# Query transposes two heads at a time, with the second copy of the rows made on GpSimd

## What is computed

```python
D_MODEL = 1024; SEQ = 1024; HEAD_DIM = 64
NSA_HEADS = 8; NSA_KV_HEADS = 2
...
def hybrid_layer(x, norm_w, w_in, q_norm_w, k_norm_w, cmp_k_pos, cmp_k_w1, cmp_k_b1, cmp_k_w2,
                 cmp_v_pos, cmp_v_w1, cmp_v_b1, cmp_v_w2, conv_w, conv_b, w_out):
    h = rms_norm(x, norm_w)
    proj = jnp.einsum('bsd,de->bse', h, w_in)
    q, kv_all, gate_logits, nsa_z, cv_h, cv_b, cv_c, cv_z = jnp.split(proj, SPLIT_POINTS, axis=-1)
    q = apply_rope(rms_norm(q.reshape(B_, S_, NSA_HEADS, dh), q_norm_w), pos)
    k_c, v_c, k_s, v_s, k_w, v_w = [t.reshape(B_, S_, G, dh) for t in jnp.split(kv_all, 6, axis=-1)]
    ...
        s_c = jnp.einsum('bgqrd,bcgd->bgqrc', qb, k_c).astype(jnp.float32) * scale
        p_c = masked_softmax(s_c, ...)
        o_cmp = jnp.einsum('bgqrc,bcgd->bgqrd', p_c.astype(v_c.dtype), v_c)
        ...
        s_s = jnp.einsum('bgqrd,bgqnld->bgqrnl', qb, k_g).astype(jnp.float32) * scale
        ...
        s_w = jnp.einsum('bgqrd,bkgd->bgqrk', qb, k_wb).astype(jnp.float32) * scale
    ...
    o_nsa = (gates[..., 0:1] * unblock(o_cmp) + gates[..., 1:2] * unblock(o_slc)
             + gates[..., 2:3] * unblock(o_win))
    o_nsa = o_nsa.reshape(B_, S_, D_NSA) * jax.nn.silu(nsa_z)
    u = cv_c * cv_h
    conv = lax.conv_general_dilated(u, conv_w[:, None, :], ...) + conv_b
    o_conv = cv_b * conv * jax.nn.silu(cv_z)
    mix = jnp.concatenate([o_nsa, o_conv], axis=-1)
    return x + jnp.einsum('bse,ed->bsd', mix, w_out)
```

## Time and profile before

| | us |
|---|---|
| median of 3 runs | 647.09 |
| lowest and highest | 646.69, 647.68 |
| the profiled execution | 648.53 |
| its span, first to last instruction | 646.7 |

### The profile page before, as it was taken

The page is one execution under the profiler, slowest core; times in us unless marked ns, Lnnn a source line. Parts: engine busy times, 40 slices in busy tenths (PEclk is TensorE's granted clock), DMA queues, the critical chain, the costliest instruction groups (busy, mean ns, idle before and its releaser), DMA issues.

```text
span 646.7 us, 10319 instructions
## 1 busy us (share of the span) xinstructions
PE 635.9 (98%) x3513; PEld 532.9 (82%) x3513; DVE 486.4 (75%) x1153; ACT 377.4 (58%) x872; POOL 203.8 (32%) x220
## 2 busy tenths in 40 slices
PE   9999999999999999999999999999999999999997
PEld 6889998888888888888877888877878888787875
DVE  4955979996745754776788867897988778888853
ACT  6754457564354444555666656668766656665651
POOL 2543304343323322423224222348742221312210
PEclk9999999999999999999999999999999999999999
DMA  8523111112111111111111010123311101011111
GB/s 299 178 57 116 34 33 50 49 35 82 32 50 33 50 33 33 36 32 34 32 34 33 17 33 18 36 89 122 116 49 56 43 34 66 33 33 50 49 34 66
DMA packets 20212, 37.35 MB, mean 58 GB/s; under 512 B 2880, under 2 KB 4288, under 8 KB 20160
## 3 DMA queue, kind: packets, MB, share of 16 engines
q1 hardware_dynamic: 20016, 36.68, 18.2%
q10 hardware_dynamic: 144, 0.00, 0.0%
HBM read 32.48 MB, written 4.19 MB: 57 GB/s over the span
## 4 chain that ended last, share of the span: by engine, by line
PE 79%; DVE 14%; issue 2%; ACT 2%; POOL 1%; DMA 1%; SPq 0%; ACTq 0%; DVEq 0%
PE pf L1478 10%; PE pf L1479 9%; PE pf L1480 9%; PE tp L1792 5%; PE sc L1632 4%; PE sc L1631 4%; PE po L1769 4%; PE po L1770 4%; PE pj L1478 3%; PE pj L1479 3%; PE pj L1480 3%; PE sc L1478 3%; PE sc L1479 3%; PE sc L1480 3%; DVE sc L1377 2%
## 5 line engine op out<-in xcount | busy, mean ns | idle before, releaser
L963 ACT CAST pth<-tp 128x512 fp32r<-128x512 f32 (+1 forms) x148 | 86.7, 586 | 102.1 <-PE tp L1792 101.6
L1377 DVE CUSTOM_DVE_ANT_0 sc<-sc,maskb 128x64 f32<-128x64 f32 (+8 forms) x192 | 103.0, 560 | 42.6 <-PE sc L1632 42.0
L1399 DVE TENSOR_TENSOR ptl<-tp,pth 128x512 fp32r<-128x512 f32 x132 | 90.9, 689 | 22.2 <-ACT pth L963 21.8
L683 POOL TENSOR_SCALAR qp<-qp,precip,gate 128x64 f32<-128x64 f32 x64 | 42.3, 661 | 182.3 <-DVE precip L1367 182.2
L643 POOL TENSOR_TENSOR fl<-fraw,fh 128x512 fp32r<-128x512 f32 x40 | 54.5, 1363 | 95.1 <-ACT fh L808 95.1
L1478 PE MATMUL pf<-hh,fh 128*128 128x512 f32 x200 | 80.2, 401 | 0.0
L1479 PE MATMUL pf<-hl,fh 128*128 128x512 f32 x200 | 78.4, 392 | 0.0
L1480 PE MATMUL pf<-hh,fl 128*128 128x512 f32 x200 | 78.2, 391 | 0.0
L634 POOL TENSOR_TENSOR wl<-qp,wh 128x512 fp32r<-128x512 f32 (+1 forms) x33 | 49.5, 1521 | 87.5 <-ACT wh L723 83.8
L1792 PEld LDWEIGHTS tp<-idr,qpr 128*128 128x128 f32 (+1 forms) x592 | 61.6, 137 | 11.9 <-issue 2.4
L1792 PE MATMUL tp<-idr,qpr 128*128 128x128 f32 (+1 forms) x592 | 68.2, 238 | 1.2 <-POOL qp L683 0.6
(11 more groups left out here) (259 smaller groups left out, 1556.8 us busy)
## 6 DMA issues: line engine op xcount, KB each, us to landing
fraw<-in_wside SPq DMA_DIRECT2D x40, 256.0 KB, 2.7
qp<-in_wpack SPq DMA_DIRECT2D x28, 256.0 KB, 3.2
xo<-in_x SPq DMA_DIRECT2D x16, 256.0 KB, 2.7
out<-xo SPq DMA_DIRECT2D x16, 256.0 KB, 2.0
wor<-in_wout SPq DMA_DIRECT2D x12, 256.0 KB, 2.8
mixc<-in_xcm SPq DMA_DIRECT2D x4, 512.0 KB, 7.4
xlow<-in_xcm SPq DMA_DIRECT2D x3, 512.0 KB, 6.8
qp<-in_wpack SPq DMA_DIRECT2D x5, 224.0 KB, 2.7
```

The source lines that it names most:

```text
L963: nc.scalar.copy(pth[ptn % 2][0:r, :], tp[tpn % 2][0:r, :]).then_inc(pth_ready, 1)
L1377: return V.tensor_tensor_reduce(row, row, mask, -1.0, -NEG, ALU.add, ALU.min, most)
L1399: V.tensor_tensor(ptl[ptn % 2][:, :], tp[tpn % 2][:, :], pth[ptn % 2][:, :].bitcast(F32), ALU.subtract).then_inc(tp_read, 1)
```

## The change

Two heads stand side by side in the 128 columns that one transpose turns, so two transposes read the normalised queries where they lie (`qpr`) and give four heads: of each pair the first head comes out in partitions 0 to 63 and the second in 64 to 127. ScalarE casts each half of the partitions into partitions 0 to 63 of `qh` (two casts of 64x256). GpSimd then copies partitions 0 to 63 of `qh` to 64 to 127 (`double_queries`), at the head of step 8u-1 (`unit_at(k, -1)`). `qd_ready` now counts that copy, and the first scores of a unit wait for it. VectorE subtracts in two pieces of 64x256 into partitions 0 to 63 of `ql`; the other half of `ql` is cleared once, before unit 0. `qd` goes. On GpSimd `last` names the semaphore and count of the instruction before the copy: the copy waits until that one is complete, and what follows waits until the copy is complete.

```diff
-                with ExitStack() as f:
-                    qdr = sb("qdr", [P, GH, 2, HD], F32R, f)
-                qd = sb("qd", [P, GH, 2, HD], F32, d)
...
@@ gpsimd
-            def copy_queries(u):
-
-                i, g = UNITS[u]
-                if u >= 1:
-                    pool.wait_ge(q_normed, 2)
-                    pool.wait_ge(qh_ready, u)
-                src = qn[:, i, g * 256:(g + 1) * 256].rearrange("p (h d) -> p h d", h=GH)
-                for twice in range(2):
-                    ins = nc.gpsimd.tensor_copy(qd[:, :, twice, :], src)
-                ins.then_inc(qd_ready, 1)
+            def double_queries(u):
+
+                pool.wait_ge(qh_ready, 2 * u + 2)
+                pool.wait_ge(*last)
+                nc.gpsimd.tensor_copy(qh[HD:P, :, :], qh[0:HD, :, :].bitcast(F32)).then_inc(qd_ready, 1)
+                pool.wait_ge(qd_ready, u + 1)
...
-            pool.wait_ge(q_normed, 1)
-            copy_queries(0)
...
+            last, scaled, low = (fl_ready, 3), 0, 0
+            double_queries(0)
             for k in range(STEPS):
+                if unit_at(k, -1):
+                    double_queries(unit_at(k, -1))
                 s = k - 1
...
-                u = unit_at(k, -5)
-                if u:
-                    copy_queries(u)
...
@@ scalar
-                nc.scalar.copy(qh[:, :, :], tp[tpn % 2][:, :].rearrange("p (h q) -> p h q", h=GH)).then_inc(qh_ready, 1)
+                pairs = qh[:, :, :].rearrange("p (j e) q -> p j e q", e=2)
+                for e in range(2):
+                    src = tp[tpn % 2][e * HD:(e + 1) * HD, 0:2 * P].rearrange("p (j q) -> p j q", j=2)
+                    nc.scalar.copy(pairs[0:HD, :, e, :], src).then_inc(qh_ready, 1)
@@ vector
-                dve.wait_ge(qh_ready, u + 1)
-                V.tensor_tensor(ql[:, :, :], tp[tpn % 2][:, :].rearrange("p (h q) -> p h q", h=GH),
-                                qh[:, :, :].bitcast(F32), ALU.subtract).then_inc(tp_read, 1)
+                pairs_h, pairs_l = (v[:, :, :].rearrange("p (j e) q -> p j e q", e=2) for v in (qh, ql))
+                for e in range(2):
+                    dve.wait_ge(qh_ready, 2 * u + e + 1)
+                    src = tp[tpn % 2][e * HD:(e + 1) * HD, 0:2 * P].rearrange("p (j q) -> p j q", j=2)
+                    ins = V.tensor_tensor(pairs_l[0:HD, :, e, :], src, pairs_h[0:HD, :, e, :].bitcast(F32), ALU.subtract)
+                ins.then_inc(tp_read, 1)
...
+            dve.wait_ge(qh_ready, 1)
+            V.memset(ql[HD:P, :, :].bitcast(F32), 0.0)
             queries(0)
@@ tensor
-                pe.wait_ge(qd_ready, u + 1)
+                pe.wait_ge(q_normed, 1 if u == 0 else 2)
                 if tpn >= 2:
                     pe.wait_ge(tp_read, tpn - 1)
-                for h in range(GH):
-                    ins = nc.tensor.transpose(tp[tpn % 2][:, h * P:(h + 1) * P].bitcast(F32R),
-                                              qdr[:, h, :, :].rearrange("p u d -> p (u d)"), idr[:, :])
+                i, g = UNITS[u]
+                for j in range(2):
+                    o = (8 + i) * 512 + (2 * g + j) * P
+                    ins = nc.tensor.transpose(tp[tpn % 2][:, j * P:(j + 1) * P].bitcast(F32R), qpr[:, o:o + P], idr[:, :])
                 ins.then_inc(tp_done, 1)
...
                 if h == 0 and w % 2 == 0:
+                    pe.wait_ge(qd_ready, w // 2 + 1)
                     pe.wait_ge(tp_read, q_tp[w // 2])
```

The remaining lines of the diff keep `last` up to date behind each GpSimd operation, for instance:

```diff
                 for h in halves_at(k):
                     half_lo(h)
+                    last = fl_ready, h + 1
```

More of the change, by code:

```diff
@@ L445, in hybrid_layer @@
         woh_ready, wol_ready = sem("woh_ready"), sem("wol_ready")
-        qd_ready, qh_ready, kend_ready = sem("qd_ready"), sem("qh_ready"), sem("kend_ready")
+        qh_ready, qd_ready, kend_ready = sem("qh_ready"), sem("qd_ready"), sem("kend_ready")
         s_done, max_ready, exp_done = sem("s_done"), sem("max_ready"), sem("exp_done")
@@ L684, in _ @@
                         .then_inc(cmp_scaled, 1)
-                u = unit_at(k, -5)
-                if u:
-                    copy_queries(u)
+                    scaled += 1
+                    last = cmp_scaled, scaled
                 u = unit_at(k, -6)
@@ L690, in _ @@
                     copy_last_keys(u)
+                    last = kend_ready, u + 1
                 for h in halves_at(k):
                     half_lo(h)
+                    last = fl_ready, h + 1
                 for j in wout_at(k):
@@ L697, in _ @@
                         .then_inc(wol_ready, 1)
+                    last = wol_ready, j + 1
                 m = mixn_half_at(k)
@@ L702, in _ @@
                                             msh[:, 0:4, :].bitcast(F32), ALU.subtract).then_inc(msl_ready, 1)
+                    low += 1
+                    last = msl_ready, low
                 m = mixc_half_at(k)
```

## The result

| | median of the runs | lowest to highest |
|---|---|---|
| before | 647.12 us | 646.69 to 647.84 (7 runs) |
| after | 649.02 us | 648.31 to 650.15 (7 runs) |

The ratio is 1.0027, with a 95% interval of 1.0017 to 1.0037, wholly above 1: the changed kernel is slower, by little. Its profiled execution took 648.31 us.

The account below looks back on a forecast made before the run. TensorE was taken as the bound (635.9 of 646.7 us busy). Terms -2.5, -0.35, +0.1, +0.36 gave -2.4, less 0.25 taken back -2.1 us: 645.0 us from the median 647.09, range 643.8 to 645.8, with A, B, D 643.7 to 647.9.

Parts of the forecast that it names:

- unit 10: Unit 10's scores start 0.2 us later behind VectorE's late subtractions, and the 0.155 us of transposes are lost: +0.36 us.
- the shorter hand-over: Transposes' end to subtraction's end shrinks by 0.07 us, gained in five units on the chain: -0.35 us.
- the transposes: TensorE: two query transposes instead of four save 0.155 us in each of 16 units: -2.5 us.
- unit 2: Unit 2's scores: spare 0.67 us, the copy needs 0.77, so TensorE waits 0.1 us.
- 0.19 more than now: ScalarE's two 64x256 casts at 0.39 us each take 0.78 us, 0.19 more than the old one.
- I allow a tenth of the saving, 0.25: VectorE's and ScalarE's longer work in the other units takes back 0.25 us of the saving.
- Rival B: VectorE gives the time back: 7 units pass on 0.165 us each, 1.2 us, giving 646.2 us; chance 0.10.
- The copy, 0.67 us: GpSimd's new 64x512 copy ahead of each unit's first scores takes 0.67 us, plus 0.1 for hand-overs.
- A: GpSimd's copy is dear, about 1.36 us; waits in units 2, 9, 11, 6, 5, 7, 10: 647.7 us; chance 0.10.
- C: Slower: first scores wait for the copy as a rule, from 1.45 us a copy on: 650.9 us; chance 0.09.
- D: The transposes save nothing, as something else sets TensorE's pace there: +0.4 us, 647.5 us; chance 0.06.
- The sum would be the same by it: The rule that VectorE and GpSimd instructions can exclude each other leaves the sum unchanged, though C would gain.

Follow-up runs that it names:

- b_again: The kernel before, unchanged, run once more for a second trace: 647.32 us.
- cast_64: before_calm with the changed kernel's two casts of 64x256, transposes, copies and the one subtraction as before: 648.97 us, 1.60 over before_calm.
- pe_only: The kernel before with two of the four query transposes from unit 2 on, nothing else touched: 646.60 us, ratio 0.9989.
- no_copy: The changed kernel without GpSimd's copy and TensorE's wait for it, upper half of `qh` zero: 649.87 us, ratio 1.0040 to the kernel before.
- after_calm: The changed kernel with GpSimd waiting in step 78 for VectorE's multiplier ahead of half 36: 648.86 us, 1.49 over before_calm.
- before_calm: The kernel before with GpSimd's subtraction `fl` of step 78 (half 36) waiting until VectorE's multiplier is done: 647.37 us.
- cast_split: The kernel before with ScalarE's query cast of 128x512 made as two of 128x256: 648.52 us, ratio 1.0020.
- sub_split: before_calm with VectorE's query subtraction made as two of 128x256 instead of one of 128x512: 647.65 us, 0.28 over before_calm.

## Why the prediction was wrong

The forecast sum was -2.1 us and the traces have +1.8: 3.9 us apart, 4.0 by the terms of the ledger. Of these, 1.4 are the path behind ScalarE's casts (+1.65, where 0.25 was allowed for ScalarE and VectorE together), 1.5 the meetings and VectorE's hold in unit 7 and at 445 us (put at nothing), 0.4 unit 10, 0.35 the shorter hand-over and 0.5 the transposes; unit 2 gives 0.1 back.

- **Transposes, -2.5 us: size nearly right.** Each pair saves 0.17 us where it stands (forecast 0.155), but in units 5, 11, 12 and 15 the turn behind the transposes waits for something else, before and after (in b_again it starts 0.41 to 0.61 us behind the first transpose, where the next matmul of the other units starts 0.29 to 0.32 behind), and nothing is saved there: 2.03 us in all.
- **ScalarE, "0.19 more than now": the term that failed.** I compared durations, 0.78 with 0.586. What queues behind a cast sees the time from start to start. That is 0.48 us for the old cast and 0.79 for the two new ones, 0.31 more.
- **"I allow a tenth of the saving, 0.25": the step that failed.** I had followed only the path from the casts to the unit's own scores, which has 0.67 us and more to spare outside unit 10. The other path from the same engine had none in several units: the exponentials and the probabilities' cast of step 8u-1, then `ptl`, then `po`. TensorE already waited there before the change, 2.6 us for `ptl` in the row of L1769 above; a wait that exists has no slack, and whatever comes ahead of it is paid in full (unit 13: 0.31 us of hold, 0.30 of wait). By cast_64 this path costs 1.6 to 2.0 us by itself. Rival B had the place in part: its sign came true, TensorE's wait for `ptl` grew from 2.6 to 4.1 us. But it gave all of it to VectorE and priced it at 1.2.
- **The shorter hand-over, -0.35 us: the time was right, the effect was none.** In unit 9 the second subtraction ends 1.29 us behind the transposes, where 1.28 was forecast and 1.35 stood before. But TensorE was idle ahead of the first scores in unit 10 alone. In units 9 and 15 the chain of the earlier trace rows goes on from `ql` through VectorE's own queue to `ptl` and `po`, and that queue sees the hold, 0.28 us longer. The ledger has no gain.
- **The copy, 0.67 us: right (0.61), and units 2, 6, 9, 11 have no wait of TensorE for it.** In unit 2 it ends 0.05 us ahead of the weight load, where a wait of 0.1 was forecast. Rivals A and C needed over 1.4 us and are out; D is out by pe_only.
- **Unit 10, +0.36: too small.** I had put the copy at 427.9, in a unit that waited for VectorE anyway. After the change VectorE is done in time, and it is the copy behind `fl`'s 1.73 us that TensorE waits for, 0.78 us:

```profile
425.40 0.73 DVE L1349 SCALAR_TENSOR_TENSOR mixc<-th,mixc 128x512 f32<-128x512 f32 x1
...
425.55 1.73 POOL L640 TENSOR_TENSOR fl<-fraw,fh 128x512 fp32r<-128x512 f32 x1
426.05 0.85 DVE L1219 TENSOR_TENSOR ql<-tp,qh 64x256 fp32r<-64x256 f32 x2
...
427.42 0.60 POOL L647 CAST qh<-qh 64x512 fp32r<-64x512 f32 x1
...
428.07 0.44 PE L1641 MATMUL sc<-kst,qh 128*128 128x384 f32 x1 [0.78 <-POOL qh L647]
```

- **"The sum would be the same by it": wrong twice.** Unit 7, VectorE's multiplier against the new copy, first b_again, then after:

```profile
343.03 0.68 DVE L1342 SCALAR_TENSOR_TENSOR mixc<-th,mixc 128x512 f32<-128x512 f32 x1
343.63 0.68 DVE L1212 TENSOR_TENSOR ql<-tp,qh 128x512 fp32r<-128x512 f32 x1
344.23 0.22 DVE L1377 CUSTOM_DVE_ANT_0 sc<-sc,maskb 128x64 f32<-128x64 f32 x1
```

```profile
341.05 0.69 POOL L647 CAST qh<-qh 64x512 fp32r<-64x512 f32 x1 [0.32 <-ACT qh L863]
341.19 1.09 DVE L1349 SCALAR_TENSOR_TENSOR mixc<-th,mixc 128x512 f32<-128x512 f32 x1
...
342.21 0.85 DVE L1219 TENSOR_TENSOR ql<-tp,qh 64x256 fp32r<-64x256 f32 x2
343.09 0.23 DVE L1384 CUSTOM_DVE_ANT_0 sc<-sc,maskb 128x64 f32<-128x64 f32 x1
```

The multiplier starts 0.14 us behind the copy and takes 0.41 us longer; the scores and `po` come late by 0.96 us in all. In no_copy the multiplier takes 0.68 us and `po` is still 0.47 us late, so the copy is about half of it. The rest fits VectorE's own hold. VectorE works without a break here, from before the casts to behind `ptl`; its next instruction starts 0.88 us behind the first of two subtractions and 0.60 us behind the single one. These 0.28 us and the 0.17 that the transposes saved ahead, which VectorE does not follow, make 0.45. ScalarE's casts by themselves do not do it: cast_64 has no such step in unit 7. No run has the changed kernel's subtractions alone, so VectorE's share is argued, not shown.

The second is at 445 us. In b_again GpSimd makes the old copies there, and VectorE's scaling beside them takes its usual time:

```profile
445.16 1.07 POOL L654 COPY qd<-qp 128x256 f32<-128x256 f32 x2
445.18 0.79 DVE L1373 TENSOR_SCALAR qp<-qp,precip,gate 128x768 f32<-128x768 f32 x1
446.19 2.52 POOL L696 TENSOR_TENSOR wol<-wor,woh 128x512 fp32r<-128x512 f32 x2
```

After, they are gone, GpSimd begins its subtraction 1 us sooner in the order, and the two start together:

```profile
444.57 2.83 POOL L692 TENSOR_TENSOR wol<-wor,woh 128x512 fp32r<-128x512 f32 x2
444.57 1.71 DVE L1380 TENSOR_SCALAR qp<-qp,precip,gate 128x768 f32<-128x768 f32 x1
```

The scaling takes 0.92 us longer and `po` waits 0.53 us more. no_copy, which also lacks the old copies, has the same (1.72 us, +0.45); cast_64 keeps them and takes 0.80. I had booked the removal of copies that nobody waits for at nothing. They kept something else away.

The Trainium skill, SBUF — State Buffer, section "SBUF: two separate sides", says that GpSimd and VectorE share a pair of ports and that the one that starts first holds it for its whole instruction; of VectorE's instructions it names those with two SBUF inputs and those in a two-port mode. The multiplier is of the first kind; whether the scaling is of the second no row says. The traces agree in kind (0.41 and 0.92 us longer), but the scaling beside the old copies in b_again was not held up (0.79 us). In the prediction I asked only whether the new instructions were of that kind, not what the moved ones would meet.
- **The base.** I took the median from the profiled execution less 1.4 us. That execution had the long meeting of unit 10, worth 1.6 us to its end, and my account of unit 10 was made from its rows, while most runs at the median do not have it. This moved the sum by little, but it made that unit's row a poor ground for the copy.

Still open: what makes a cast of 64x256 hold ScalarE for 0.39 us where one of 128x256 holds it for 0.27 (narrowed down below), the 0.5 us between the traces and the medians (1.49 us by medians, 1.98 by one trace each, for after_calm over before_calm), and how the loss of unit 7 divides.

## What to carry to other kernels

- Price an instruction on a strict queue by the distance from its start to the next start, taken from the trace, and follow every path that leaves the engine behind it, first those on which the bounding engine already waits: there the slack is zero, and the 0.3 us are paid in full, as in units 13 and 14 here.
- Removing or moving an instruction that nobody waits for is not free. It lets its successors start sooner, and where GpSimd and VectorE then run together, one of them can take longer (0.41 us, 0.92 us and 1.06 us here).
- Before a difference of 2 us is explained from two traces, find out whether two executions of the same kernel differ by as much, and make the comparison in one order of events. The same goes for an experiment's own edit: two subtractions of another shape had the right duration and the wrong hold. Where a change pays in some units and not in others, it can be made in those alone.

## What the runs showed of the hardware that I had not expected

| form | duration of one | first start to next instruction's start |
|---|---|---|
| ScalarE's cast, one of 128x512 | 586 ns | 0.48 us |
| two of 128x256 (cast_split) | 375 ns | 0.53 us |
| two of 64x256, the second from the upper partitions (cast_64, after) | 368 ns | 0.77 to 0.79 us |
| VectorE's subtraction, one of 128x512 | 689 ns | 0.60 to 0.61 us |
| two of 128x256 (sub_split) | 418 ns | 0.67 us |
| two of 64x256, the second from the upper partitions (after) | 420 ns | 0.88 to 0.89 us |

Casts of the same number of columns and nearly the same duration hold the engine for 0.27 or 0.39 us each. In the first two rows the next instruction starts 0.11 to 0.12 us ahead of the cast's end, in the third it starts 0.02 to 0.03 us behind it, and the second cast starts 0.01 to 0.02 us behind the end of the first. VectorE shows the same.

No run tried this by itself, but other instructions of ScalarE in the trace after narrow it down:

```profile
109.80 0.58 ACT L774 COPY mixn<-pj 64x512 f32<-64x512 f32 x1 [2.14 <-PE pj L1489]
110.39 0.58 ACT L775 COPY mixn<-pj 64x512 f32<-64x512 f32 x1
110.99 1.08 ACT L786 CAST kst<-xt 128x512 fp32r<-128x512 f32 x2
...
507.55 0.58 ACT L967 CAST pth<-tp 64x512 fp32r<-64x512 f32 x1 [1.53 <-PE tp L1803]
508.04 0.31 ACT L955 ACTIVATE qp<-sc,nmax 128x64 f32<-128x64 f32 x1
```

The cast of L967 covers 64 partitions, and the next instruction starts 0.1 us ahead of its end: the number of partitions alone is not it. L774 and L775 write unbroken rows and have no overlap: the stride of the output alone is not it either. What these pairs without overlap have in common is that the input or the output starts at another partition than in the instruction in front: L775 writes from partition 64 on, between two that write from 0 on; the second query cast reads from 64 on, between two that read from 0 on. On VectorE two subtractions of 64x512 in a row that both read and write from partition 64 on (L1099, `kst`) do overlap: 0.69 us each, 0.61 from start to start. So it is the change that goes with the lost overlap, not the upper half as such. This is what the trace shows; no run changed this alone.

GpSimd copies 64 partitions of 512 columns to the other half in 0.60 to 0.61 us undisturbed, less than half of its two-input subtraction of 512 columns.
